# Down product of a dense feed-forward layer: one product over all rows against seven products of half matrices

## The reference

```python
def swiglu_ffn(h, w_gate_up, w_down):
    gate, up = jnp.split(jnp.einsum("bsd,df->bsf", h, w_gate_up), 2, axis=-1)
    return jnp.einsum("bsf,fd->bsd", jax.nn.silu(gate) * up, w_down)
...
ffn = swiglu_ffn(rms_norm(h, norm_ffn_pre[l]), w_gate_up[l], w_down[l])
h = h + rms_norm(ffn, norm_ffn_post[l])
```

## Time and profile before

| what | value |
|---|---|
| median of three runs | 2109.79 us |
| the profiled execution: its own time | 2109.43 us |
| its span | 2107.6 us |
| PE busy | 2060.8 us, 98% of the span |
| DVE busy, ACT busy | 1520.3 us (72%), 1381.6 us (66%) |
| share of PE in the chain that ended last | 93% |
| mean granted clock of PE | 0.993 |
| the down product on PE | 546.24 to 665.9 us |

### The profile page before, as it was taken

One profiled execution on the slowest core, in us unless ns is written; L12 is line 12 of the kernel. 1 busy time (PEld: TensorE's weight loads), 2 busy tenths in 40 slices (PEclk: granted clock), 3 DMA queues, 4 the chain that ended last, 5 costly groups with the idle time before them and its releaser, 6 DMA issues.

```text
span 2107.6 us, 31365 instructions
## 1 busy us (share of the span) xinstructions
PE 2060.8 (98%) x10497; PEld 1709.1 (81%) x10497; DVE 1520.3 (72%) x1713; ACT 1381.6 (66%) x1870; POOL 194.8 (9%) x232
## 2 busy tenths in 40 slices
PE   7999999999999999899999999999999999999998
PEld 6888888888887887678888888888888888888877
DVE  4357643323334777789898989898989999898984
ACT  3258643222224447388888888888888888888863
POOL 0000000000000000111111111111111111111110
PEclk9999999999999999899999999999999999999999
DMA  6321023222322320589999999999999999999971
GB/s 200 130 76 61 21 71 113 97 100 80 120 100 88 125 81 21 211 299 377 371 369 379 360 370 368 368 371 365 373 369 375 366 374 362 367 372 369 370 272 40
DMA packets 86559, 511.24 MB, mean 243 GB/s; under 512 B 17286, under 2 KB 18906, under 8 KB 29147
## 3 DMA queue, kind: packets, MB, share of 16 engines
q1 hardware_dynamic: 71312, 487.61, 61.5%
q0 software_dynamic: 9680, 17.33, 3.2%
q10 hardware_dynamic: 5498, 5.39, 0.9%
HBM read 503.44 MB, written 23.07 MB: 250 GB/s over the span
## 4 chain that ended last, share of the span: by engine, by line
PE 93%; DVE 2%; issue 2%; ACT 2%; DMA 1%; ACTq 0%; POOL 0%; SPq 0%; POOLq 0%; DVEq 0%
PE PS L2615 17%; PE PS L2617 17%; PE PS L2616 17%; PE PS L255 10%; PE PS L257 10%; PE PS L256 10%; PE PS L1154 1%; PE PS L2498 1%; PE PS L2612 1%; PE PS L2625 1%; PE PS L1885 1%; PE PS L1086 1%; PE PS L1818 1%; PE PS L1811 0%; PE PS L749 0%
## 5 line engine op out<-in xcount | busy, mean ns | idle before, releaser
L2492 DVE TENSOR_TENSOR WL<-RING,WH 128x2048 fp32r<-128x2048 f32 x385 | 873.6, 2289 | 96.2 <-ACT WH L2472 93.0
L2472 ACT ACTIVATE WH<-RING 128x1024 fp32r<-128x1024 f32 x770 | 805.9, 1059 | 161.9 <-PE PS L2617 156.2
L2615 PE MATMUL PS<-WH,RA 128*128 128x512 f32 x1540 | 629.1, 409 | 2.1 <-ACT AR L2523 2.1
L2617 PE MATMUL PS<-WH,RA 128*128 128x512 f32 x1540 | 601.0, 390 | 0.0
L2616 PE MATMUL PS<-WL,RA 128*128 128x512 f32 x1540 | 600.7, 390 | 0.0
L2617 PEld LDWEIGHTS PS<-WH,RA 128*128 128x128 f32 x1540 | 289.6, 188 | 61.8
L2615 PEld LDWEIGHTS PS<-WH,RA 128*128 128x128 f32 x1540 | 290.9, 189 | 57.6 <-issue 2.2
L2616 PEld LDWEIGHTS PS<-WL,RA 128*128 128x128 f32 x1540 | 290.2, 188 | 58.2
L255 PE MATMUL PS<-WH,RA 128*128 128x512 f32 (+1 forms) x560 | 219.2, 391 | 3.1 <-DVE WL L245 1.9
L257 PE MATMUL PS<-WH,RA 128*128 128x512 f32 (+1 forms) x560 | 215.6, 385 | 0.0
L256 PE MATMUL PS<-WL,RA 128*128 128x512 f32 (+1 forms) x560 | 215.4, 385 | 0.0
(11 more groups left out here) (395 smaller groups left out, 2249.0 us busy)
## 6 DMA issues: line engine op xcount, KB each, us to landing
RING<-w_experts SPq DMA_DIRECT2D x390, 1024.0 KB, 7.3
RING<-w_front SPq DMA_DIRECT2D x58, 1024.0 KB, 4.8
X<-x SPq DMA_DIRECT2D x4, 512.0 KB, 5.7
acc_scr<-X SPq DMA_DIRECT2D x4, 512.0 KB, 5.4
xs_scr<-AR SPq DMA_DIRECT2D x4, 512.0 KB, 3.2
X<-acc_scr SPq DMA_DIRECT2D x4, 512.0 KB, 5.4
out<-X SPq DMA_DIRECT2D x8, 256.0 KB, 2.0
RING<-w_front SPq DMA_DIRECT2D x2, 816.0 KB, 4.4
```

What stands on the lines that cost most here:

```text
L2472: e.activation(WH[:, m % 3, v], RING[:, m % 6, v], ACT.Copy).then_inc(s("m_hi"), 1)
L2492: e.tensor_tensor(WL[:, m % 3, :], RING[:, m % 6, :], WH[:, m % 3, :].bitcast(F32), ALU.subtract).then_inc(s("m_lo"), 1)
L2615: e.matmul(PS[bank][:, :], lhs[0][:, kr + k, :], WH[:, m % 3, c], start=(sel is None and kr == 0 and k == 0), stop=False)
L2617: x = e.matmul(PS[bank][:, :], lhs[1][:, kr + k, :], WH[:, m % 3, c], start=False, stop=(stop and k == 3))
```

## The change

The hidden matrix is cut into halves by tokens (256 + 256) and by inner columns (11 + 11 tiles), `w_down` by rows (11 + 11 tiles) and by output columns (512 + 512). In place of eight products of such blocks there are seven, with sums of blocks as operands. Each product is 11 tiles deep, two token tiles high and 512 columns wide, and is done in three steps of 4, 4 and 3 tiles; a step has one chunk of weights and meets only two token tiles.

- The sums of weight blocks are made during gate and up: POOL issues a load of four blocks (w_down laid out for it), DVE makes four sums (`dve_weight_sums`, in f = 2 to 7), and POOL issues four stores to a scratch tensor in memory. SP loads those chunks from there.
- The sums of hidden blocks are made by DVE (`dve_hidden_sum`): six before or in the first step, three after steps 3, 4 and 5, three after steps 8, 9 and 10.
- Products leave PSUM one at a time: two copies on ACT and twelve additions of 128x512 on DVE (`dve_down_out`), between the splits.
- Hidden rows have four half-size buffers instead of two. Order on ACT and DVE in step st: hidden rows of step st+1, then the weights of step st+3, then what else is listed for st.
- Token tiles 2 and 3 end with product 6 (of 7): their norm, residual and transposes stand between steps 18 and 20, those of tiles 0 and 1 inside mix2's first product.

```diff
-DOWN_ROWS = ((0, 2), (2, 4), (6, 4), (10, 4), (14, 4), (18, 4))
+DOWN_ROWS = ((0, 4), (4, 4), (8, 3))
+DOWN_PRODUCTS = (("A11", 0, 0), ("S2", None, 3), ("A12", 1, 0), ("S3", None, 1), ("S1", None, 0), ("A22", None, 2), ("S4", 1, 512))
+DOWN_STEPS = [(p, r) for p in range(7) for r in range(3)]
+DOWN_BANKS = (4, 6, 0, 2, 4, 6, 0)
+DOWN_BUFS = [0, 2, 1, 3] * 4 + [2, 3, 0, 1, 0]
...
+            for st in range(21):
+                pe_down(e, st)
+
+        def pe_down(e, st):
...
+            e.wait_ge(s("w_lo"), ch.split + 1)
+            e.wait_ge(s("v_hs"), st + 1)
+            for half in range(2):
...
...
+                x.then_inc(s("p_pr"), 1)
+            if st == 19:
+                pe_joint_T(e, 1, "mix2", 2, [X[:, i, :] for i in range(4)])
+                pe_joint_T(e, 1, "mix2", 3, [X[:, i, :] for i in range(4)])
...
+        def dve_late_add(e, i):
+            e.wait_ge(s("g_r4"), jpow(1, "P", i))
+            e.wait_ge(v_c.sem, v_c.n)
+            e.scalar_tensor_tensor(X[:, i, :], JJ[i], R4[:, i:i + 1], X[:, i, :], ALU.mult, ALU.add).then_inc(s("v_x"), 2)
...
+            for st in range(20):
+                if st == 0:
+                    dve_hidden_sum(e, 4)
+                    dve_hidden_sum(e, 5)
+                dve_hidden(e, st + 1)
+                dve_split(e, 39 + st)
+                if st in (3, 4, 5):
+                    dve_hidden_sum(e, st + 3)
+                if st in (8, 9, 10):
+                    dve_hidden_sum(e, st + 1)
+                for half in range(2):
+                    if st == 6:
+                        dve_down_out(e, 1, half, U2[half], R1[half], "a_r1", "v_u2")
+                    if st == 12:
+                        dve_down_out(e, 3, half, U3[half], U2[half], "v_u2", "v_u3")
+                    if st == 15:
+                        dve_down_out(e, 4, half, JJ[2 + half][:, 512:1024], U3[half], "v_u3", "v_cc")
+                        dve_down_out(e, 4, half, U2[half], U2[half], "v_u3", "v_u4")
+                    if st == 16:
+                        dve_down_out(e, 2, half, JJ[half][:, 0:512], R1[half], "a_r1", "v_c11")
+                    if st == 18:
+                        dve_down_out(e, 5, half, JJ[2 + half][:, 0:512], U3[half], "v_u3", "v_cc")
...
+                if st == 18:
+                    for i in (2, 3):
+                        dve_late_mean(e, i)
+                        dve_late_gain(e, i)
+                    for i in (2, 3):
+                        dve_late_add(e, i)
...
+            for c, i in ((61, 2), (61, 3), (62, 2), (62, 3), (61, 0), (61, 1), (62, 0), (62, 1)):
+                e.wait_ge(s("w_lo"), CH[c].split + 1)
+                e.wait_ge(s("v_xt"), XT["mix2"] + 2 * LATE.index(i) + 2)
+                pe_tile(e, c, i, H0[i], c == 61, c == 62)
+                if (c, i) == (62, 2):
+                    pe_joint_T(e, 1, "mix2", 0, XT4)
+                    pe_joint_T(e, 1, "mix2", 1, XT4)
-            free = {0: [("a_z", 1)], 1: [("v_z", 1)], 2: [("a_z", 2)], 3: [("v_z", 2)]}
+            free = {0: [("a_z", 2)], 1: [("v_z", 2)], 2: [("a_z", 1)], 3: [("v_z", 1)]}
```

More of the change, by code:

```diff
@@ L83, in front_chunks @@
         columns("w_gate_up", [(256 * f, 256), (FF + 256 * f, 256)], 4, gain=8)
-    both("w_down", DOWN_ROWS)
+    for _, half, block in DOWN_PRODUCTS:
+        for k0, nk in DOWN_ROWS:
+            if half is None:
+                out.append(Chunk("sums", k0, nk, [(block, 512)], 2))
+            else:
+                out.append(Chunk("w_down", 11 * half + k0, nk, [(block, 512)], 2))
     for grp in (0, 1, 3, 2):
@@ L98, in front_chunks @@
         ch.done = outs
-        ch.at, at = at, at + 128 * ch.nk * ch.w
+        ch.at, at = at, at + (0 if ch.src == "sums" else 128 * ch.nk * ch.w)
         ch.split = None
@@ L217, in sp_load @@
             n = ch.nk * ch.w
+            if ch.src == "sums":
+                e.wait_ge(s("d_ts"), 16 * 4 * len(SUM_ROWS))
+                e.dma_start(RING[:, ch.slot, 0:n].rearrange("p (k n) -> p k n", k=ch.nk),
+                            sum_d[ch.cols[0][0], ch.k0:ch.k0 + ch.nk].rearrange("k p n -> p k n")).then_inc(s(f"w_ld{ch.slot}"), 16)
+                return
             e.dma_start(RING[:, ch.slot, 0:n], A["w_front"][ch.at:ch.at + 128 * n].rearrange("(p n) -> p n", p=128)
@@ L419, in act_joint @@
                 high(3)
-            else:
-                out(0)
-                out(1)
-                out(2)
-                high(0)
-                out(3)
-                for i in range(1, 4):
-                    high(i)
-                for i in range(4):
-                    sums(i)
         def dve_out_gain(e, p, c, half, i, GROW):
@@ L485, in dve_joint @@
                 low(3)
-            else:
-                out(0)
-                add(0)
-                out(1)
-                add(1)
-                out(2)
-                low(0)
-                add(2)
-                out(3)
-                low(1)
-                add(3)
-                low(2)
-                low(3)
-                for i in range(4):
-                    mean(i)
         def pe_joint_T(e, p, stage, i, XR):
@@ new lines, in hidden_ready, with hidden_free @@
+        def hidden_ready(e, st):
+            p, r = DOWN_STEPS[st]
+            name, (k0, nk) = DOWN_PRODUCTS[p][0], DOWN_ROWS[r]
+            if name == "A11":
+                e.wait_ge(s("v_hid"), k0 + nk)
+            elif name[0] == "A":
+                e.wait_ge(s("v_hid"), 22)
+            else:
+                e.wait_ge(s("v_ss"), DOWN_SUMS.index((name, r)) + 1)
+        def hidden_free(e, st):
+            z = DOWN_BUFS[st]
+            before = [q for q in range(st) if DOWN_BUFS[q] == z]
+            e.wait_ge(s("p_pr"), CH[40 + before[-1]].done if before else CH[38 + z % 2].done)
@@ new lines, in act_late_high, with dve_late_low @@
+        def act_late_high(e, i):
+            for half in range(2):
+                e.wait_ge(s("p_xt"), XT["mix2"] + 2 * LATE.index(i) + half + 1)
+                e.activation(XP[0][:, 4 * half:4 * half + 4, 128 * i:128 * i + 128],
+                             PS[TBK[1][i][half]][:, :].rearrange("p (k n) -> p k n", k=4), ACT.Copy).then_inc(s("a_xt"), 1)
+        def dve_late_low(e, i):
+            for half in range(2):
+                v = (slice(None), slice(4 * half, 4 * half + 4), slice(128 * i, 128 * i + 128))
+                e.wait_ge(s("a_xt"), XT["mix2"] + 2 * LATE.index(i) + half + 1)
+                e.tensor_tensor(XP[1][v], PS[TBK[1][i][half]][:, :].rearrange("p (k n) -> p k n", k=4), XP[0][v].bitcast(F32),
+                                ALU.subtract).then_inc(s("v_xt"), 1)
@@ L1459, in dve_ffn @@
                 else:
+                    for n in range(4):
+                        dve_hidden_sum(e, n)
                     dve_hidden(e, 0)
+                if 2 <= f < 8:
+                    dve_weight_sums(e, f - 2)
                 for m in range(2):
@@ new lines, in dve_ffn @@
+            dve_late_low(e, 2)
+            dve_late_low(e, 3)
+            for half in range(2):
+                dve_down_out(e, 6, half, JJ[half][:, 512:1024], U2[half], "v_u4", "v_cc")
+            for i in range(2):
+                dve_late_mean(e, i)
+                dve_late_gain(e, i)
+            for i in range(2):
+                dve_late_add(e, i)
+            for i in range(2):
+                dve_late_low(e, i)
+            for i in LATE:
+                dve_late_norm(e, i)
+            dve_split(e, 59)
@@ L3036, in _ @@
                 pool_joint(e, 0)
+                pool_weight_sums(e)
                 pool_joint(e, 1)
@@ L3095, in laid_out @@
     for ch in chunks:
+        if ch.src == "sums":
+            continue
         rows = inputs[ch.src][0][ch.k0 * 128:(ch.k0 + ch.nk) * 128]
@@ L3099, in laid_out, with laid_out_sums @@
     return np.concatenate(parts)
+def laid_out_sums(w):
+    blocks = w.reshape(2, 11, 128, 2, 512).transpose(0, 3, 1, 2, 4).reshape(4, 11, 128, 512)
+    return np.concatenate([blocks[:, k0:k0 + nk].transpose(2, 0, 1, 3).reshape(-1) for k0, nk in SUM_ROWS])
 def laid_out_experts(inputs):
```

297 lines of the change are left out of this document (195 added, 102 removed).

## The result

The changed kernel takes **2121.19 us** (median of five runs, 2119.51 to 2121.92), the kernel before 2109.79 us beside it (2106.23 to 2111.33): a ratio of 1.0050, with a 95% interval of 1.0039 to 1.0062. It is slower, by more than the 0.2% that a measurement tells from no change. The forecast was 2118.5 us. The profiled execution took 2120.03 us.

The account below looks back on a forecast made before the run. PE was taken as the bound, busy 98% of the span. -15.0 + 16.1 + 8.0 = 9.1 at the product's end, 7.5 after mix2, 9.1 with the clock, on 2109.43: 2118.5 us, own range 2113.5 to 2124 (62%), overall 2109 to 2126.

Parts of the forecast that it names:

- 66 matmuls, -15.0: Down product on PE: 462 matmuls instead of 528, at 0.2267 us each, save 15.0 us.
- Waits inside the product, +16.1: Down product: PE waits for hidden rows behind the next step's weights on DVE, 14 waits, together 16.1 us.
- The stand, +8.0: Between steps 19 and 20: PE stands 8.0 us for tiles 2 and 3's norm and residual, 16 transposes inside.
- The clock, +1.6: At step 20: one slow stretch after the idle time, eight matmuls by 0.2 us, 1.6 us; bounds 0 and 3.2.
- The end of the product: Down product on PE: ends at 675.0, 9.1 us later than before, without the slow clock.
- ACT's last split: Mix2: ACT's last split of transposed rows ends at 686.3 instead of 678.13, 8.1 us later, without the slow clock.
- The same four sums, eleven transfers and the same work of DVE.: Mix2, behind ACT's last split: this work stays the same, so DVE reaches line 1768 just 8.1 us later.
- The short wait that I had named as a sign for mix2: Mix2: sign of being right, PE waits shortly at chunk 56 for line 1768's successor; 0.66 us spare there.
- a clock under 1.00 in more than one place: Sign of being wrong: the windows show a granted clock under 1.00 more than once.
- Nothing later gives it back.: After mix2: PE's 7.5 us of lateness stays to the end, since later work runs on the same three engines.
- Sums of weights at nothing: Gate and up, f = 2 to 7: the weight sums, 19.3 us, hide under PE's 21.8 us per f, costing nothing.
- the one that would have made it faster: Rival: ACT and DVE run ahead, no waits inside the product, 2102.4 us; 10%.

Follow-up runs that it names:

- e8_before_less: Kernel before, with 66 matmuls of the down product left out and no order, wait or addition changed: 2097.8 us, ratio 0.9921 to the kernel before.
- e10_best: Changed kernel, hidden rows two steps ahead, tail reordered, second product added out of PSUM at step 14 (not 16), chunk 64's split earlier: 2095.6 us, ratio 0.9912.
- e1_ahead: Changed kernel, with hidden rows of step st+2 (not st+1) split ahead of the weights of step st+3: 2109.5 us, ratio 0.9989 to the kernel before.
- e5_fill: Changed kernel, with eight matmuls on constants put into PE's stand between steps 19 and 20: 2119.5 us, ratio 1.0033 to the kernel before.
- e12_load_behind: Changed kernel, with SP's load of chunk 66 held until the second mixer's eleven small transfers have landed: 2116.6 us, ratio 1.0037 to the kernel before.
- e9_no_weight_sums: Changed kernel, without forming or storing sums of weight blocks, as many bytes loaded from the weights' array instead: 2123.4 us, ratio 1.0052 to the kernel before.
- e3_both: Changed kernel, with hidden rows two steps ahead and tiles 2 and 3's norm earlier, their transposes behind step 20: 2103.2 us, ratio 0.9953 to the kernel before.
- e11_split60: Changed kernel, with the split of chunk 64's weights ahead of ACT's and DVE's waits for small transfers: 2116.8 us, ratio 1.0031 to the kernel before.
- e4_positions: Changed kernel, with the positions' transfer moved from last to first of the second mixer's eleven small transfers: 2122.2 us, ratio 1.0043 to the kernel before.

## Why the prediction was right

The sign and the range came out as forecast, and so did the mechanism up to the end of the product; in mix2 it was another one. The steps one by one:

- **66 matmuls, -15.0.** Right: -16.7 with an interval that holds it, and a product 15.0 us shorter in the trace (e8_before_less); a product of 104.7 us in e10_best.
- **Waits inside the product, +16.1.** From 546.57 to the end of step 19 at 662.68 + 0.23 are 116.3 us, with 444 matmuls of 0.2267 (100.7) in them: 15.7. The first wait ends at 553.26 (forecast 553.05), the longest at 647.15 with 2.30 (forecast 647.28). e1_ahead shows that they are of order. This was the surest part, since each hand-over had a row.
- **The stand, +8.0.** From 662.91 to 671.96 are 9.05 us. The 16 transposes in it take 3.33, where at the full clock they take 1.67 (685.17 to 686.84), so 7.4 are the stand's.
- **The clock, +1.6.** The slow stretch came where it was put, but it slowed the transposes too: 1.66 there, and 0.97 in step 20 (677.01 - 671.96 = 5.05 against 4.08), 2.6 together; e5_fill gets 2.3 back. The rule of the Trainium skill ("TensorE: Matmul & The Clock Gate", Part 1) that I weighed there, that activity releases the throttle and idleness brings it back, agrees with this stand (granted 0.69 and 0.63 behind it), though not with every wait (last section).
- **The end of the product.** 677.01 against 650.98 + 16.1 + 8.0 + 1.6 = 676.7, and the 0.33 between them is a later first matmul. That it fits so closely is partly luck: the waits came 0.4 and the stand 0.6 under their terms, and the clock 1.0 over its own.
- **ACT's last split.** +9.7, forecast 8.1 + 1.6 = 9.7.
- **"The same four sums, eleven transfers and the same work of DVE."** This step failed. I moved the row of transfers as a block and gave it the wait of before, 5.46 us. It was 8.28. The load beside it is what costs (5.26 without it, e12_load_behind); why before it cost next to nothing, with the load 0.50 us behind the issue and not 0.32, isn't shown. That is 2.8 us, and it turned the wait that I had put at the successor of line 1768, 0.66 us spare in all, into one of 3.42 us at chunk 64's weights, an instruction group earlier on DVE, with a second slow stretch (0.69) that had no term. The short wait that I had named as a sign for mix2 didn't come, and one of my signs of being wrong did: a clock under 1.00 in more than one place (665 to 675 and 715 to 720 us).
- **"Nothing later gives it back."** Wrong by 1.5 us: 12.1 us late on PE in mix2's diff stage (785.18 against 773.11), 11.2 at the second gather, 10.6 at the end. In the routing PE stands and runs at the low clock in both kernels, only in other windows (granted 0.57 from 880 to 900 us and 1.00 from 900 to 920 before, 0.72 and 0.85 in the changed kernel).
- **Sums of weights at nothing.** Right, as far as the intervals of e9_no_weight_sums tell.

Against 2109.43 + 9.1 the profiled execution came 1.5 us later, the two misses partly cancelling, which is luck too. Of the rivals, the one that would have made it faster named the right fact, that ACT and DVE have time enough, and e1_ahead and e10_best are what it takes to use it.

## What to carry to other kernels

When a change makes steps shorter, the passes that refill buffers for each step keep their length, so look first at what stands between "buffer free" and "next step may start" on each engine, and put the short operand of the next step ahead of the pass that waits for a buffer. A saving of 15 us by fewer matmuls became a loss of 11 by such orders, and a gain of 14 to 19 by four moves that removed no work. Count, with every wait of TensorE, whether it brings a slow stretch behind it; and don't move a row of small transfers as a block without asking which large load lands beside it.

## What the runs showed of the hardware that I had not expected

- The same wait of 1.97 us, in the same place and for the same line, left the granted clock at 1.00 in e1_ahead (640 to 645 us) and took it to 0.70 in e3_both, where it cost 1.85 us more. The waits of up to 2.30 us inside the changed product cost none. The window of e1_ahead, then that of e3_both:

```profile
640.00:645.00 5.00, 5.00 (x24) 4.10 (x23) 4.11 (x5) 1.05 (x4) 0.00 (x0) 1.00 0.67 231
```

```profile
640.00:645.00 5.00, 5.00 (x17) 3.99 (x17) 4.06 (x5) 0.00 (x0) 0.00 (x0) 0.70 0.74 298
```

- Sixteen passes over constants, 5.3 us in a stand of 5.7, held the clock at 1.00 (e5_fill).
- The last of eleven small transfers took 5.5 us from issue to use with a 1 MB load held back (e12_load_behind), and 8.6 to 9.0 us in the six kernels where that load was issued 0.31 to 0.35 us behind. At 0.50 us it took 5.9 to 7.2 us in four kernels and 8.9 us in a fifth (e11_split60), so the distance alone doesn't settle it. Sending another of them last, with the load in front of its issue, left DVE waiting 7.93 us (e4_positions).
- The same kernel differs by 0.2% between chips (2110 to 2114 us for the kernel before), as much as the effects of several of these edits. Only ratios on one chip tell them apart.
